# One-hot tiles of the late retrieval steps in bf16, in three exact weight parts, with the low parts of the table all on GpSimd

## What is computed

```python
def peer_mixer(h, w_q, sub_keys, u_tab, v_tab):
    q = (xb @ w_q).reshape(tb, 8, 2, 128)
    s = einsum('thpd,hpnd->thpn', q, sub_keys)
    s_top, i_top = top_k(s, 16)                  # of 128 keys, in each half
    cand = s_top[:, :, 0, :, None] + s_top[:, :, 1, None, :]
    best, pos = top_k(cand, 16)                  # 16 of 16 x 16 pairs
    idx = i_top[..., 0] * 128 + i_top[..., 1]    # of the chosen pairs
    g = softmax(best)
    act = gelu(einsum('thkd,td->thk', u_tab[idx], xb))
    return einsum('thk,thkd->td', g * act, v_tab[idx])
```

## Time and profile before

| | |
|---|---|
| median of three runs | 2136.32 us (2133.85 to 2136.97) |
| the profiled execution, its own time | 2135.08 us |
| its span (first to last instruction) | 2132.9 us |
| mean granted TensorE clock | 0.988 of full speed |
| HBM read, mean rate over the span | 449.93 MB, 215 GB/s |

### The profile page before, as it was taken

One profiled execution on the slowest core, in us unless ns is written; L12 is line 12 of the kernel. 1 busy time (PEld: TensorE's weight loads), 2 busy tenths in 40 slices (PEclk: granted clock), 3 DMA queues, 4 the chain that ended last, 5 costly groups with the idle time before them and its releaser, 6 DMA issues.

```text
span 2132.9 us, 40134 instructions
## 1 busy us (share of the span) xinstructions
PE 2067.8 (97%) x14238; PEld 1834.4 (86%) x14238; DVE 1501.6 (70%) x2698; ACT 1250.6 (59%) x2232; POOL 802.0 (38%) x569
## 2 busy tenths in 40 slices
PE   6999899999999999999998989999999999999998
PEld 3778899999999987777778879999999997777776
DVE  3436579736777778878778563996588887787785
ACT  3534444545666667767754634545566666676774
POOL 1010047754555522223302400688366652222330
PEclk9999999999999999999999989999999999999999
DMA  9745447775555678888864544456544447888883
GB/s 346 278 159 178 151 143 251 239 267 196 188 191 189 201 237 294 296 303 297 296 209 127 153 142 149 147 183 192 189 143 143 138 146 261 299 299 296 297 301 114
DMA packets 125494, 459.95 MB, mean 216 GB/s; under 512 B 14016, under 2 KB 14544, under 8 KB 124352
## 3 DMA queue, kind: packets, MB, share of 16 engines
q1 hardware_dynamic: 102976, 377.14, 52.9%
q0 software_dynamic: 21504, 79.53, 10.1%
q10 hardware_dynamic: 896, 1.76, 0.2%
HBM read 449.93 MB, written 8.44 MB: 215 GB/s over the span
## 4 chain that ended last, share of the span: by engine, by line
PE 92%; DVE 4%; DMA 2%; ACT 1%; issue 1%; SPq 0%; POOL 0%; DVEq 0%; ACTq 0%
PE pu L1332 12%; PE pu L1337 11%; PE pm L1408 11%; PE pm L1410 11%; PE pm L1409 11%; PE pu L1333 11%; PE pu L1202 4%; PE pu L1203 4%; PE pu L1204 4%; PE pm L1367 3%; PE pm L1366 2%; PE pm L1224 1%; PE pm L1672 1%; DMA arena<-in_ada 1%; DVE w_lo L1732 1%
## 5 line engine op out<-in xcount | busy, mean ns | idle before, releaser
L778 ACT ACTIVATE w_hi<-raw 128x1024 fp32r<-128x1024 f32 x600 | 634.0, 1057 | 445.7 <-PE pm L1410 225.4
L1732 DVE TENSOR_TENSOR w_lo<-raw,w_hi 128x1024 fp32r<-128x1024 f32 x444 | 572.3, 1289 | 388.2 <-ACT w_hi L778 377.3
L1332 PE MATMUL pu<-hid_split,w_hi 128*128 128x256 f32 x2048 | 500.3, 285 | 0.0
L1333 PE MATMUL pu<-hid_split,w_hi 128*128 128x256 f32 x2048 | 492.4, 280 | 0.0
L1408 PE MATMUL pm<-w_hi,hid_split 128*128 128x512 f32 x1024 | 405.0, 396 | 3.1 <-DVE hid_split L1995 3.1
L1332 PEld LDWEIGHTS pu<-hid_split,w_hi 128*128 128x128 f32 x2048 | 386.3, 189 | 24.5 <-issue 24.5
L1410 PE MATMUL pm<-w_lo,hid_split 128*128 128x512 f32 x1024 | 403.7, 394 | 0.0
L1409 PE MATMUL pm<-w_hi,hid_split 128*128 128x512 f32 x1024 | 402.9, 394 | 0.0
L1333 PEld LDWEIGHTS pu<-hid_split,w_hi 128*128 128x128 f32 x2048 | 386.1, 189 | 0.0
L577 POOL TENSOR_TENSOR w_lo<-raw,w_hi 128x1024 fp32r<-128x1024 f32 x96 | 229.9, 2396 | 188.4 <-ACT w_hi L778 188.4
L1337 PE MATMUL pu<-hid_split,w_lo 128*128 128x256 f32 x2048 | 290.5, 284 | 0.1
(11 more groups left out here) (276 smaller groups left out, 2931.5 us busy)
## 6 DMA issues: line engine op xcount, KB each, us to landing
raw<-in_u_tab SPq DMA_DIRECT2D x256, 512.0 KB, 3.6
raw<-in_v_tab SPq DMA_DIRECT2D x256, 512.0 KB, 3.5
raw<-in_ada SPq DMA_DIRECT2D x80, 512.0 KB, 3.7
raw<-in_wq SPq DMA_DIRECT2D x32, 512.0 KB, 3.5
raw<-in_gla_in SPq DMA_DIRECT2D x24, 512.0 KB, 4.7
raw<-in_rg_in SPq DMA_DIRECT2D x20, 512.0 KB, 3.5
arena<-in_ada SPq DMA_DIRECT2D x8, 1024.0 KB, 16.7
arena<-in_gla_state POOLq DMA_DIRECT2D x8, 512.0 KB, 14.0
```

The lines of the kernel that those rows point to most:

```text
L778: act.activation(w_hi[:, s2, :], raw[:, s4, :], ACT.Copy).then_inc(hi_done, 1)
L1332: mm(pu[:, s, 0:SEQ], w_hi[:, s % 2, kk * P:kk * P + P], hid_hi[:, kk, 0:SEQ], start=(kk == 0), stop=False)
L1333: mm(pu[:, s, 0:SEQ], w_hi[:, s % 2, kk * P:kk * P + P], hid_lo[:, kk, 0:SEQ], start=False, stop=False)
L1732: tt_(w_lo[:, s2 if l2 is None else l2, :], raw[:, s4, :], w_hi[:, s2, :].bitcast(F32), ALU.subtract).then_inc(lo_done, 1)
```

## The change

- `oh_b` (second one-hot) and the weighted first one-hot are bf16 tiles. The latter, `oh_w`, has three parts in place of the two fp32r tiles `oh_hi` and `oh_lo`: each weight is split into three bf16 parts whose sum is exact. Every row that a matmul reads is 128 contiguous elements.
- Late step of TensorE: three bf16 matmuls per token in place of two fp32r ones.
- Late step of VectorE: the two comparisons have bf16 inputs and outputs, with a bf16 copy of the key numbers and the indices from SBUF (`pair_s`, each index stored twice side by side); `times_rest` makes parts two and three of `oh_w`, two products per step, with the weights' parts, also stored twice, from PSUM (`part_p`). It makes no low part in the late steps.
- Late step of GpSimd: the low part of every step, in one instruction, and nothing else.
- Late step of ScalarE: scales by the first part, into bf16; `gelu_in_place` stands ahead of `high`.
- Once per token tile: seven more small VectorE instructions that make the parts, five transposes in place of three. Once per layer: nine copies in place of a copy and a subtraction.

```diff
-POOL_ALL = POOL_LOWS + LATE // 2
+POOL_ALL = POOL_LOWS + LATE
...
-        oh_b = sb("oh_b", [P, TOKS, NKEY], F32R)
-        oh_hi = sb("oh_hi", [P, TOKS, NKEY], F32R)
+        oh_b = sb("oh_b", [P, TOKS, NKEY], BF16)
+        oh_w = sb("oh_w", [P, 3, TOKS, NKEY], BF16)
+        iota_b = sb("iota_b", [P, NKEY], BF16)
+        ident_b = sb("ident_b", [P, P], BF16)
...
+        pair_s = nc.alloc_sbuf_tensor_at("pair_s", [P, 2 * KD, 2 * T], BF16, offset=hid_at)[:, :, 2 * SEQ:2 * T]
...
+        pair_p = pm[:, 0, SEQ:2 * SEQ].bitcast(BF16).rearrange("p (a n) -> p a n", a=2)
+        part_p = pm[:, 1, :].bitcast(BF16).rearrange("p (a n d) -> p a n d", a=2, d=2)
...
-                def low_part(i, c, slot, part):
-                    half = slice(part * (D // 2), part * (D // 2) + D // 2)
+                def late_low(i, c, slot):
                     pool.wait_ge(hi_done, i * 4 + (m0 + EARLY + c + 1))
-                    last = pool.tensor_tensor(w_lo[:, c % 2, half], raw[:, slot, half], w_hi[:, c % 2, half].bitcast(F32),
-                                              ALU.subtract)
...
+                    pool.tensor_tensor(w_lo[:, c % 2, :], raw[:, slot, :], w_hi[:, c % 2, :].bitcast(F32),
+                                       ALU.subtract).then_inc(lo_pool, 1)
...
                     act.wait_ge(split_used, i * 4 + (m0 + EARLY + c + 1))
+                    gelu_in_place(c)
                     if lay == 0:
                         slot, full = u_load(0, EARLY + c + 2)
                         high(slot, c % 2, full)
                     else:
                         high((c + 2) % 4, c % 2, i * 16 + (full0 + EARLY * 4 + (c + 2) // 4 * 16))
-                    gelu_in_place(c)
...
+                    for a in range(2):
+                        pe.transpose(pair_p[:, a, tt * P:tt * P + P], part_b[:, a, :], ident_b[:])
+                        pe.transpose(pm[:, 1, a * SEQ + tt * P:a * SEQ + tt * P + P], part_d[:, a, :], ident)
+                    last = pe.transpose(pm[:, 0, tt * P:tt * P + P], part_f[:, 0, :], ident)
...
-                        mm(out, oh_b[:, t, :], oh_hi[:, t, :], start=True, stop=False)
-                        last = mm(out.rearrange("p (a n) -> p a n", a=4), oh_b[:, t, :], oh_lo[:, t], start=False, stop=True)
+                        for part in range(3):
+                            last = mm(out, oh_b[:, t, :], oh_w[:, part, t, :], start=(part == 0), stop=(part == 2))
...
+                    dve.tensor_copy(part_b[:, 0:2, :], slot[:, 0:2, :])
+                    link(dve.tensor_copy(part_2[:, :, 0], slot[:, 2, :]))
+                    link(dve.tensor_copy(part_f[:, 0, :], part_2[:, :, 0]))
+                    link(tt_(part_f[:, 1, :], slot[:, 2, :], part_f[:, 0, :], ALU.subtract))
+                    link(dve.tensor_copy(part_2, bc(part_f[:, 1, :], P, SLOTS, 2)))
+                    link(dve.tensor_copy(part_f[:, 2, :], part_2[:, :, 0]))
+                    tt_(part_3, bc(part_f[:, 1, :], P, SLOTS, 2), bc(part_f[:, 2, :], P, SLOTS, 2),
+                        ALU.subtract).then_inc(slot_ready, 1)
...
+                dve.tensor_copy(sel_w[:], pm[:, 0, 0:SEQ])
+                for a in range(2):
+                    for c in range(4):
+                        src = pair_p[:, a, :].rearrange("p (i c t) -> p c t i", c=4, t=TOKS)[:, c]
+                        last = dve.tensor_copy(
+                            pair_s[:, c * TOKS:c * TOKS + TOKS, a * 32:a * 32 + 32].rearrange("p t (i d) -> p t i d", d=2),
+                            src.unsqueeze(3).to_broadcast([P, TOKS, 16, 2]))
...
-                    tt_(oh_eq[:], numbers, bc(pm[:, 1, bass.ds(i * 16 + c * TOKS, TOKS)], P, TOKS, NKEY),
-                        ALU.is_equal).then_inc(eq_ready, 1)
+                    tt_(by_two(oh_eq[:]), numbers, key_of(i, c, 0), ALU.is_equal).then_inc(eq_ready, 1)
...
+                    tt_(by_two(oh_b[:]), numbers, key_of(i, c, 1), ALU.is_equal).then_inc(ob_ready, 1)
+
+                def times_rest(i, c):
+
+                    dve.wait_ge(eq_ready, i * 4 + (g0 + c + 1))
+                    for part in range(2):
+                        last = tt_(by_two(oh_w[:, part + 1]), by_two(oh_eq[:]), weight_of(i, c, part), ALU.mult)
+                    last.then_inc(oh_lo_ready, 1)
...
                     if final < 2:
                         second_hot(i, c + 1)
-                    if c % 2 == 0:
-                        low(i * 4 + (m0 + EARLY + c + 1), slot, 1)
+                        times_rest(i, c + 1)
```

More of the change, by code:

```diff
@@ L320, in build_step @@
         eps_set = sem("eps_set")
+        iota_set = sem("iota_set")
         hid_full = sem("hid_full")
@@ L620, in late_two @@
-                def late_two(i, c, slot, final=False):
-                    times_low(i, c + 1)
-                    if not final:
-                        low_part(i, c + 2, slot, 0)
-                        times_low(i, c + 2)
-                        low_part(i, c + 2, slot, 1)
-                times_low(0, 0)
-                for part in range(2):
-                    low_part(0, 0, u_load(lay, EARLY)[0], part)
+                    pool.tensor_tensor(w_lo[:, c % 2, :], raw[:, slot, :], w_hi[:, c % 2, :].bitcast(F32),
+                                       ALU.subtract).then_inc(lo_pool, 1)
@@ L1942, in peer, with key_of, weight_of, by_two @@
                 dve.wait_ge(slot_t, lay * 2 + 2)
-                link(dve.tensor_copy(sel_w[:, 0, 0:SEQ], pm[:, 0, 0:SEQ]))
-                tt_(sel_w[:, 1, 0:SEQ], pm[:, 0, 0:SEQ], sel_w[:, 0, 0:SEQ].bitcast(F32), ALU.subtract).then_inc(sel_ready, 1)
-                numbers = iota.unsqueeze(1).to_broadcast([P, TOKS, NKEY])
+                dve.tensor_copy(sel_w[:], pm[:, 0, 0:SEQ])
+                for a in range(2):
+                    for c in range(4):
+                        src = pair_p[:, a, :].rearrange("p (i c t) -> p c t i", c=4, t=TOKS)[:, c]
+                        last = dve.tensor_copy(
+                            pair_s[:, c * TOKS:c * TOKS + TOKS, a * 32:a * 32 + 32].rearrange("p t (i d) -> p t i d", d=2),
+                            src.unsqueeze(3).to_broadcast([P, TOKS, 16, 2]))
+                link(last)
+                dve.nop().then_inc(sel_ready, 1)
+                numbers = iota_b[:].rearrange("p (x d) -> p x d", d=2).unsqueeze(1).to_broadcast([P, TOKS, NKEY // 2, 2])
+                def key_of(i, c, a):
+                    at = pair_s[:, c % 4 * TOKS:c % 4 * TOKS + TOKS, bass.ds(i * 2 + (a * 32 + c // 4 * 2), 2)]
+                    return at.unsqueeze(2).to_broadcast([P, TOKS, NKEY // 2, 2])
+                def weight_of(i, c, part):
+                    return part_p[:, part, bass.ds(i * 16 + c * TOKS, TOKS), :].unsqueeze(2).to_broadcast(
+                        [P, TOKS, NKEY // 2, 2])
+                def by_two(tile):
+                    return tile.rearrange("p t (x d) -> p t x d", d=2)
                 def first_hot(i, c):
```

76 lines of the change are left out of this document (29 added, 47 removed).

## The result

The changed kernel takes 2143.63 us (median of 7 runs, 2140.85 to 2146.41) against 2135.61 us (7 runs, 2133.85 to 2136.97) on the same chip: a ratio of 1.0038, 95% interval 1.0026 to 1.005. It is slower by 8 us (0.4%, clear of the interval), where 2 us less were forecast. The profiled execution took 2144.81 us with a span of 2143.0, 10.1 more than the span of before.

A forecast was written before the change was run, and what follows sets the result against it. TensorE, busy 97% of the span, was taken as the bound. Layer 1 late steps +3.2, layer 0 -6.4 and 0, the exponential's chain +1.4: -1.8, say -2 us, so 2134 us; range 2108 to 2180, about 0.8.

The forecast's parts named there:

- TensorE's part: Late steps: 12 bf16 one-hot matmuls at 0.059 us replace 8 fp32r; 0.20 us saved per step, unstalled step 3.52.
- Comparisons and products in pairs: VectorE, late steps: 16-bit elements taken two at once, so 512 elements cost 0.42 us.
- that rival: Late steps: products with weights from PSUM don't go in pairs, 1.20 us for two instead of 0.68; 2180 us, 12%.
- The wait of the comparisons behind GpSimd: Layer 1 late steps: comparisons reading two SBUF inputs wait out GpSimd's low part; step 3.77 against 3.72, +3.2 us.
- Layer 0: Late steps: 32 steps with an adaLN chunk go from 4.46 to 4.26 us, -6.4 us; the 32 others 0.
- about 2 us a tile at 0.28 each ... the 4 us are hidden there: Routing: seven small VectorE instructions per token tile, two tiles, fit in VectorE's idle time before ScalarE's exponential; no cost.
- the rule for VectorE instructions with two SBUF inputs: Such an instruction waits out a GpSimd instruction that reads SBUF, then needs its own stream only.
- the 11.80 us of cover: Layer 1: VectorE's idle time until ScalarE's exponential, taken to hide the routing's added instructions; 8.81 us in layer 0.
- lost cover: Without VectorE's idle time before the exponential, the routing's added 4 us would stand on the path.
- The chain behind the exponential: Layer 1, VectorE from the exponential to its first low part: added copies, products and a wait, +1.4 us on TensorE's path.
- the packed comparisons don't wait: Late steps: 16-bit comparisons don't wait for GpSimd, the step stays 3.52 us; -24 us, 2112 us, 17%.

The follow-up runs named there:

- experiment 1: The changed kernel with the row of key numbers that both comparisons read copied into PSUM in layer 1: 2127.94 us, ratio 0.9964.
- experiment 8: The changed kernel with GpSimd's low part of each late step made as two instructions of 512 columns: 2120.81 us, ratio 0.9933.
- experiment 2: The changed kernel with the scratch tiles of the routing weights' split held in PSUM: 2138.49 us, ratio 1.002.
- experiment 3: The changed kernel with the low parts of early steps 48 to 51 on GpSimd too: 2138.61 us, ratio 1.002.
- experiment 10: The changed kernel with GpSimd's early low parts as two instructions of 512 columns each, late ones whole: 2140.69 us, ratio 1.003.
- 5: The changed kernel with key numbers in PSUM in layer 1, weight split through PSUM and low parts 48 to 51 on GpSimd: 2119.55 us, ratio 0.9922.
- experiment 9: The changed kernel with GpSimd's late low parts in two instructions, weight split through PSUM, low parts 48 to 51 on GpSimd: 2112.89 us, ratio 0.9903.
- experiment 7: The changed kernel with the odd late steps' low parts back on VectorE, GpSimd doing only the even ones: 2152.35 us, ratio 1.0077.
- experiment 4: The changed kernel with ScalarE's late-step order undone, high part ahead of the gelu: 2152.53 us, ratio 1.0086.
- experiment 6: The kernel of experiment 5's three edits with ScalarE's order undone as well, high part ahead of the gelu: 2121.35 us, ratio 0.9933.

## Why the prediction was wrong

**TensorE's part: right, a little short.** The one-hot block took 0.63 us of weight loads (12 x 0.053, forecast 12 x 0.059), and the gap ahead of it grew, so that the unstalled step is 3.55 and not 3.52: 0.17 saved per step, not 0.20. The Trainium skill's 81 ns for a sustained stream with 128 columns (TensorE: Matmul & The Clock Gate, Back-to-back issue gap) does not hold here; the trace shows 53 ns.

**Comparisons and products in pairs: right.** 0.41 us for 512 elements, key or weight in PSUM or not. The Trainium skill's tier table (VectorE: DVE Perf Modes, The perf-mode tier table) would have made the products 0.68 and that rival true; the trace is with its other section, Why PSUM operands drop a tier.

**The wait of the comparisons behind GpSimd: right in mechanism and place, undersized.** Forecast was a hand-carried pattern of 3.52, 3.78, 4.07 with 3.77 taken; the trace has 3.57, 3.83, 4.0 to 4.2, mean 3.822. Layer 1 lost 6.4 instead of 3.2. Experiment 1 shows that nothing else is in it, experiment 8 that it goes when GpSimd's instruction is half as long.

**Layer 0: right sum (-6.2 for -6.4) by two errors that cancel.** The chunk steps went from 4.46 to 4.31, not 4.26 (31 x 0.15 = 4.7), and the others from 3.755 to 3.710 where I had 0 (32 x 0.045 = 1.4).

**The step that failed: "about 2 us a tile at 0.28 each ... the 4 us are hidden there".** The prediction states the rule for VectorE instructions with two SBUF inputs and then prices seven SBUF instructions beside GpSimd's early passes as if they ran free. Two of the seven have two SBUF inputs, and the trace adds what the rule as I had written it left out: casts with one SBUF input wait as well (2.29 and 2.46 us). 8.5 us a tile overran the 11.80 us of cover, VectorE came 2.8 us late to the exponential, and the next things late were those named for lost cover: TensorE at the transposes of step 20 and at the low part of step 48, and with it the clock. Experiments 2, 3 and 10 take this apart; 5 and 9 bring the stretch back to 183.0. The chain behind the exponential itself, +1.4 in the prediction, measured +1.6. The Trainium skill (SBUF — State Buffer, Who interferes with whom), the same page that I had cited for the rule, does name them: copies and casts can run in a two-port mode and then contend for the shared pair too. By that, the trace agrees.

**What was in no term.** 3.0 us between the layers. There the same sixteen matmuls ran for part of their time at the lower of the clock's two levels (granted clock 0.68 from 1110 to 1115 us; 1.00 in experiment 1 from 1111 to 1121):

```profile
1111.68 5.81 PE L1195 MATMUL pm<-arena 128*128 128x288 f32 x16 [1.04 <-ACT arena L808]
```

against, with the clock up, experiment 1, whose program differs from the changed kernel up to that place by one wait:

```profile
1115.66 4.12 PE L1196 MATMUL pm<-arena 128*128 128x288 f32 x16 [1.03 <-ACT arena L809]
```

That is 1.7 of the 3.0; most of the rest are the projection matmuls behind them, which stay at the lower clock for 6.0 us in place of 3.8. Over the thirteen profiles that stretch took 221.4 to 224.6 us, without order by edit. What decides it stays open, and so does whether the other executions of the changed kernel had it. It is not needed for the verdict: the early and late steps of layer 1 lose 13.8 us, less the 6.2 of layer 0.

Of the rivals, "the packed comparisons don't wait" (2112 us) was false as a forecast, and its number is about what removing the waits gives: 2112.9 in experiment 9. That the two times meet to 1 us is in part luck: the rival's sum was 24 us less than the kernel before, with steps of 3.52 and 1.4 us lost ahead of them; experiment 9 is 22 us under its own kernel before, with steps of 3.553 and nothing lost.

## What to carry to other kernels

When a VectorE instruction is to run beside GpSimd elementwise work, list for every instruction, small ones in a routing or set-up chain too, whether it touches SBUF alone (two inputs, or a copy or cast); each such one can cost the rest of a GpSimd instruction, and its price is not its own length. Move one operand to PSUM, or cut the GpSimd instruction into pieces; in the late steps either turned a loss of 8 us into a gain of 7 to 14, while in the short chain of the split the pieces did less than PSUM. A VectorE whose busy time rises when its work was cut is the sign to look for, and idle time is cover only once the waits inside the new work have been added up.

## What the runs showed that I had not expected

- One-input casts from SBUF to SBUF wait for GpSimd like two-input operations (2.29 us for 128 elements, 0.23 alone; in experiment 3 an f32 copy of 32 elements, 2.19 in place of 0.17), while copies from SBUF to PSUM (0.28 to 0.43), reductions and the top-16 search did not.
- Half as many GpSimd passes took away only a quarter of the comparisons' waiting (experiment 7: 2.1 us for each pass against 1.4), since the engines' queues settled into a repeating pattern in which each pass is met at its start. A mere swap of two ScalarE instructions made the late steps 6 us longer (experiment 4) or left them as they were (experiment 6).
- GpSimd is held up in return: a pass of 1024 columns takes 2.38 us when no comparison reads SBUF alone, 2.49 in the changed kernel, and 2.7 in halves.
- A wait of 4.3 us on TensorE was followed by granted clocks of 0.81 and 0.77, and the next matmuls and the next interval took 0.6 and 1.2 us longer. After a wait of 2.04 us (experiment 2) the clock stayed at 1.00, but after one of 1.84 us (experiment 10) the eight `w_lo` matmuls took 1.71 us again: the length of the wait alone does not tell it.
